# Attention's output normalised ahead of its split, the MLP norm's sum inside the third opening product, and another order of the maxima

## What is computed

```python
def rmsnorm(x, g):
    y = x * lax.rsqrt(jnp.mean(x * x, axis=-1, keepdims=True) + EPS)
    return y * g

def layer_output(x, q_nope, q_pe, pos, ckv_keys, kpe_keys, key_pos, y_lru, p):
    ...
    o = chunk_causal_attention(...)                    # softmax(q k) v, 8 heads of 64
    merged = jnp.concatenate([rmsnorm(o.reshape(B, T, ATTN_W), p["attn_out_g"]),
                              rmsnorm(y_lru, p["lru_out_g"])], axis=-1)
    h = x + merged @ p["w_out"]
    f = jnp.square(jax.nn.relu(rmsnorm(h, p["norm_mlp_g"]) @ p["w_up"])) @ p["w_down"]
    return h + f
```

## Time and profile before

| | us |
|---|---|
| median of 3 runs | 2449.06 (2448.76 to 2449.34) |
| the profiled execution | 2446.93 |
| its span, first to last instruction | 2445.1 |
| PE, DVE, ACT, POOL busy | 2427.2, 1806.5, 1283.4, 537.9 |
| granted TensorE clock, mean | 0.999 of 2.4 GHz |
| attention of the first layer, about | 297 to 457 |
| its Y products | 457 to 501 |
| its output products | 501 to 548 |
| its first MLP products | 548 to 574 |

### The profile page before, as it was taken

The page is one execution under the profiler, slowest core; times in us unless marked ns, Lnnn a source line. Parts: engine busy times, 40 slices in busy tenths (PEclk is TensorE's granted clock), DMA queues, the critical chain, the costliest instruction groups (busy, mean ns, idle before and its releaser), DMA issues. The chain is left out here.

```text
span 2445.1 us, 44182 instructions
## 1 busy us (share of the span) xinstructions
PE 2427.2 (99%) x17358; PEld 2340.8 (96%) x17358; DVE 1806.5 (74%) x2893; ACT 1283.4 (52%) x2306; POOL 537.9 (22%) x513
## 2 busy tenths in 40 slices
PE   9999999999999999999999999999999999999998
PEld 9999977899999999999999999778999999999998
DVE  8677767778776677677686777687787766776676
ACT  5566355655554454455535763557455544554454
POOL 0024155200112211220201142552002112211212
PEclk9999999999999999999999999999999999999999
DMA  4232200453447634664731221005435456546655
GB/s 164 71 115 73 53 11 20 88 154 106 96 86 139 129 84 98 133 120 90 221 100 52 61 73 54 11 20 115 133 109 114 88 115 132 109 87 121 132 104 185
DMA packets 109740, 242.48 MB, mean 99 GB/s; under 512 B 15536, under 2 KB 18960, under 8 KB 109408
## 3 DMA queue, kind: packets, MB, share of 16 engines
q0 software_dynamic: 48512, 102.26, 23.3%
q1 hardware_dynamic: 60880, 137.37, 18.0%
q10 hardware_dynamic: 144, 0.04, 0.0%
HBM read 147.39 MB, written 94.29 MB: 99 GB/s over the span
## 5 line engine op out<-in xcount | busy, mean ns | idle before, releaser
L3270 DVE TENSOR_TENSOR wlo<-raw_all,whi 128x512 fp32r<-128x512 f32 (+1 forms) x420 | 270.6, 653 | 181.1 <-ACT whi L2308 178.6
L2308 ACT ACTIVATE whi<-raw_all 128x512 fp32r<-128x512 f32 (+1 forms) x420 | 248.6, 599 | 278.4 <-DVE raw_all L3403 88.0
L3792 POOL DMA_DIRECT2D x_scratch<-stage x224 | 200.0, 943 | 839.1 <-DVE stage L3413 694.0
L2361 ACT ACTIVATE stage<-ps 128x536 f32<-128x536 f32 (+1 forms) x224 | 135.5, 612 | 148.6 <-PE ps L1590 143.6
L3413 DVE TENSOR_TENSOR stage<-stage,ps 128x536 f32<-128x536 f32 (+1 forms) x168 | 118.9, 708 | 84.8 <-PE ps L1590 84.0
L2873 DVE TENSOR_REDUCE mxp<-ps 128x1 f32<-128x80 f32 (+10 forms) x376 | 137.1, 376 | 51.7 <-PE ps L1304 47.7
L1113 PE MATMUL ps<-xgh,whi 128*128 128x358 f32 (+1 forms) x720 | 157.2, 326 | 0.0
L1113 PE MATMUL ps<-xgl,whi 128*128 128x358 f32 (+1 forms) x720 | 156.6, 325 | 0.0
L1113 PE MATMUL ps<-xgh,wlo 128*128 128x358 f32 (+1 forms) x720 | 156.5, 325 | 0.0
L1738 ACT ACTIVATE whi<-raw_all 128x1024 fp32r<-128x1024 f32 (+3 forms) x64 | 58.1, 908 | 174.5 <-PE ps L1113 158.0
L1113 PEld LDWEIGHTS ps<-xgl,whi 128*128 128x128 f32 x720 | 124.0, 189 | 0.0
(11 more groups left out here) (948 smaller groups left out, 7799.7 us busy)
## 6 DMA issues: line engine op xcount, KB each, us to landing
raw_all<-in_wst SPq DMA_DIRECT2D x237, 256.0 KB, 3.4
raw_all<-in_wst SPq DMA_DIRECT2D x74, 512.0 KB, 3.6
x_scratch<-stage POOLq DMA_DIRECT2D x120, 268.0 KB, 6.1
x_scratch<-stage POOLq DMA_DIRECT2D x120, 264.0 KB, 6.0
xall<-x_scratch SPq DMA_DIRECT2D x32, 537.0 KB, 8.6
x_scratch<-xall POOLq DMA_DIRECT2D x24, 537.0 KB, 3.5
raw_all<-in_wst POOLq DMA_DIRECT2D x30, 256.0 KB, 5.5
xall<-in_xT SPq DMA_DIRECT2D x8, 537.0 KB, 8.4
```

Of the source, the lines that this page charges most:

```text
L2308: nc.scalar.activation(dst, src, ACT.Copy).then_inc(S["u_hi"], 1)
L2361: nc.scalar.activation(quarters(stage_of(L, g, i, n)[:, 0:N2]), src, ACT.Copy, scale=-1.0 if row else 1.0).then_inc(S["x_copy"], 1)
L3270: V.tensor_tensor(dst, src, hi.bitcast(F32), ALU.subtract).then_inc(S["u_lo"], 1)
L3792: pool.dma_start(x_scr[2 * i + row, :, a:b], stage_of(L, g, i, n)[:, 0:b - a], accum_op=ALU.add).then_inc(S[done], 16)
```

## The change

Four things, in both layers.

1. In attention, DVE's copy of bank 1's sums moves from step 12 to step 13, behind `all_parts` and `shift_lo`, and `invert` of heads 2, 4 and 6 from step 10 to step 14. The last reciprocal, after head 7, moves ahead of the first Y weight parts.
2. Attention's output is divided by its root-mean-square before the split: `divide(3)`, the squares and their sum come earlier, PE sums after P7 of pair 2, ACT makes logarithm and root around the copy of P4 of pair 2, DVE multiplies o by the root (`o_normal`, four operations, new), ACT rounds and DVE makes the low parts after that. The output products are then added to x straight from PSUM, one DVE operation each and not two.
3. Some of ACT's PSUM copies in the Y stage stand ahead of weight roundings, others behind.
4. The sum for the MLP norm is made from two fp32r parts (ACT rounds, L2261 of the changed file; DVE makes the rest), after 3 of the 8 tiles of the third opening product.

```diff
+SUM_LAG = [OUT_LAG, OUT_LAG + 1, OUT_LAG]
...
-INVERT_AT = 10
+INVERT_AT = 14
...
 # PE
                     if u in (U_OO, U_OO + 1):
                         w("y_copy", y_copied(u - U_OO + 2, "P4"))
                         w("y_add", y_added(3, "P3"))
-                        w("root", SUM_O)
...
                     if name == "P1":
+                        if p == 3:
+                            w("root", SUM_O)
...
-                        if (p, name) == (NYP - 1, "P7"):
+                        if (p, name) == (2, "P7"):
                             w("sum_lo", SUM_O)
...
                             sum_of_parts(SUM_O, osqt_r, osq_r)
...
-                pe.wait_ge(S["xm_sum"], L * PER["xm_sum"] + 7)
-                sum_of_squares(SUM_MLP, xss)
                 pe.wait_ge(S["u_lo"], L * PER["u_lo"] + 4)
                 pe.wait_ge(S["p_copy"], L * PER["p_copy"] + 2)
-                first_up(2, range(8), True)
+                first_up(2, range(3), False)
+                w("sum_lo", SUM_MLP)
+                sum_of_parts(SUM_MLP, xss_hi, xss_lo)
+                first_up(2, range(3, 8), True)
...
 # ACT, Y stage, from pair 1's P6 on
                 y_copy(1, "P6")
-                o_high(2)
                 y_fill_hi(2, 1)
-                o_square(2)
+                o_square(3)
                 y_fill_hi(2, 2)
                 y_copy(1, "P4")
-                y_fill_hi(2, 3)
+                w("o_sum", 3)
+                nc.scalar.activation(live(osqt_r), live(osq), ACT.Copy).then_inc(S["sum_hi"], 1)
                 y_copy(2, "P1")
-                o_high(3)
+                y_fill_hi(2, 3)
                 y_copy(2, "P5")
                 y_fill_hi(3, 0)
                 y_copy(2, "P6")
-                o_square(3)
                 y_fill_hi(3, 1)
-                y_fill_hi(3, 2)
+                log_sum(SUM_O, rs, ATT)
                 y_copy(2, "P4")
-                y_fill_hi(3, 3)
+                exp_root(SUM_O, rs)
+                y_fill_hi(3, 2)
                 y_copy(3, "P1")
-                w("o_sum", 3)
-                nc.scalar.activation(live(osqt_r), live(osq), ACT.Copy).then_inc(S["sum_hi"], 1)
+                y_fill_hi(3, 3)
+                o_high(0)
+                o_high(1)
                 y_copy(3, "P5")
                 split(B_OO)
                 y_copy(3, "P6")
-                log_rstd(SUM_O, rs, ATT)
+                o_high(2)
+                o_high(3)
                 split(B_OO + 1)
                 y_copy(3, "P4")
...
 # DVE
-                            hb, ib = divmod(h * NP + i - OUT_LAG - BANK_LAST[n_bank], NP)
+                            hb, ib = divmod(h * NP + i - SUM_LAG[n_bank] - BANK_LAST[n_bank], NP)
...
+                def o_normal(j):
+
+                    w("rstd", SUM_O)
+                    w("o_sq", j + 1)
+                    V.tensor_tensor(live(o[j]), live(o[j]), live(rs), ALU.mult).then_inc(S["o_n"], 1)
...
+                divide(3)
                 y_add(1, "P2")
                 y_add(1, "P7")
...
+                o_add(3)
                 y_add(1, "P3")
-                divide(3)
                 y_fill_lo(2, 2)
+                sum_lo(osq_r, osq, osqt_r, SUM_O)
...
                 y_add(2, "P3")
+                o_normal(0)
                 y_fill_lo(3, 2)
+                o_normal(1)
                 y_fill_lo(3, 3)
-                o_low(3)
-                sum_lo(osq_r, osq, osqt_r, SUM_O)
+                o_low(0)
+                o_normal(2)
                 split(B_OO)
+                o_normal(3)
                 y_add(3, "P2")
                 y_add(3, "P7")
+                o_low(1)
                 y_add(3, "P3")
+                o_low(2)
+                o_low(3)
                 split(B_OO + 1)
...
-                    scaled(U_OO + i, osqt, rs, "oo_ev", LIVE)
-                    w("oo_ev", i + 1)
                     w(f"x_in{m}", 32)
-                    V.tensor_tensor(live(x[m]), live(x[m]), live(osqt), ALU.add).then_inc(S["res_add"], 1)
+                    w("mm", U_OO + i + 1)
+                    V.tensor_tensor(chunks(x[m], LIVE), chunks(x[m], LIVE), slot(U_OO + i, LIVE), ALU.add).then_inc(S["res_add"], 1)
```

More of the change, by code:

```diff
@@ L250 @@
 for _c in range(8):
-    READ[U_OO + _c] = ("oo_ev", _c + 1)
+    READ[U_OO + _c] = ("res_add", _c + 1)
 for _c in range(10):
@@ L612, in trunk @@
                 seven[name, kk] = [part[:, h * HALF:(h + 1) * HALF] for part in b_in[m]]
+        xss_lo, xss_hi = place("xss_lo", "G", PIECE * 6, TOK, F32R), place("xss_hi", "G", PIECE * 4, TOK, F32R)
         xss, xsq = place("xss", "G", PIECE * 6, TOK), [place(f"xsq{n}", "G", PIECE * (2 + 2 * n), TOK) for n in range(2)]
@@ L666, in trunk @@
             *((f"x_in{m}", 32) for m in range(8)), ("x_out", 32 * 8), *((f"staged{i}", 0) for i in range(N_STAGE)), ("xg_hi", 8), ("xg_lo", 8), ("sq", 8), ("sq_sum", 7),
-            ("root", 6), ("rstd", 6), ("sum_hi", 5), ("sum_lo", 5),
+            ("root", 6), ("rstd", 6), ("sum_hi", 6), ("sum_lo", 6),
             ("xr_ev", 4), ("xr_raw", 0), ("conv", 4), ("xc_hi", 4), ("xc_lo", 4),
@@ L716, in sum_rest @@
             if n in (SUM_O, SUM_MLP):
-                return ps[:, 1 if n == SUM_O else 5, CH:CH + b - a - SUM_END]
+                return ps[:, 5, CH:CH + b - a - SUM_END]
             return ps[:, 3 * slot_of(sum_at(n, layer)) + 2, CH:CH + b - a - SUM_END]
@@ L1480, in _ @@
                 pe.wait_ge(S["u_lo"], L * PER["u_lo"] + 2)
-                pe.wait_ge(S["oo_ev"], L * PER["oo_ev"] + 7)
+                pe.wait_ge(S["res_add"], L * PER["res_add"] + 7)
                 first_up(0, range(6), False)
-                pe.wait_ge(S["oo_ev"], L * PER["oo_ev"] + 8)
+                pe.wait_ge(S["res_add"], L * PER["res_add"] + 8)
                 first_up(1, range(6), False)
@@ L1809, in log_rstd, with exp_root @@
                     nc.scalar.activation(dst[:, a + SUM_END:b], sum_rest(n, L), ACT.Ln, scale=1.0 / dim, bias=eps[:, 0:1]).then_inc(S["root"], 1)
+                def exp_root(n, dst):
                     w("root", n)
+                    a, b = sum_cols(n, L)
                     nc.scalar.activation(dst[:, a:b], dst[:, a:b], ACT.Exp, scale=-0.5).then_inc(S["rstd"], 1)
+                def log_rstd(n, dst, dim):
+                    log_sum(n, dst, dim)
+                    exp_root(n, dst)
                 w("vec_in", 16)
@@ L2080, in o_high @@
                 def o_high(j):
-                    w("o", j + 1)
+                    w("o_n", j + 1)
                     nc.scalar.activation(live(oh[j]), live(o[j]), ACT.Copy, scale=col(V_AG + j)).then_inc(S["o_hi"], 1)
                 def o_square(j):
+                    w("o", j + 1)
                     if j >= 2:
@@ L2092, in _ @@
                 y_copy(0, "P1")
-                o_high(0)
+                o_square(0)
                 y_copy(0, "P5")
@@ L2096, in _ @@
                 y_copy(0, "P6")
-                o_square(0)
+                o_square(1)
                 y_fill_hi(1, 1)
-                o_high(1)
-                o_square(1)
                 y_copy(0, "P4")
@@ L2104, in _ @@
                 y_fill_hi(1, 3)
+                o_square(2)
                 y_copy(1, "P5")
@@ L2244, in opening @@
                     w("res_add", 8)
+                    w("xm_sum", 7)
+                    nc.scalar.activation(xss_hi[:, A0:TOK], xss[:, A0:TOK], ACT.Copy).then_inc(S["sum_hi"], 1)
                     copy_out(at, 0, True)
@@ L3065, in _ @@
                 y_add(0, "P3")
-                o_low(0)
+                o_add(1)
                 y_fill_lo(1, 2)
                 y_block_sum(2, 0)
-                o_add(1)
                 y_fill_lo(1, 3)
+                o_add(2)
                 y_fill_lo(2, 0)
                 y_block_sum(2, 1)
-                o_low(1)
+                divide(3)
                 y_add(1, "P2")
@@ L3168, in _ @@
                 for i, m in enumerate(OO_ORDER):
-                    if i == 0:
-                        w("rstd", SUM_O)
                     if i == 6:
@@ L3194, in _ @@
                 in_sum(7)
-                for name, kk in F_ORDER[2:]:
+                for name, kk in F_ORDER[2:4]:
+                    seven_sum(name, kk)
+                w("sum_hi", SUM_MLP)
+                lo(xss_lo[:, LIVE[0]:TOK], xss[:, LIVE[0]:TOK], xss_hi[:, LIVE[0]:TOK], "sum_lo")
+                for name, kk in F_ORDER[4:]:
                     seven_sum(name, kk)
```

24 lines of the change are left out of this document (9 added, 15 removed).

## The result

The changed kernel takes 2471.64 us (median, 2470.58 to 2473.03), the kernel before in the same session 2448.76: ratio 1.0095, 95% interval 1.0081 to 1.0109. That is 22.9 us slower. The forecast was slower too, but by 9.2 us (2458.3), and the measured time lies above its range (2451 to 2463) and above every rival, D included.

What follows compares the result with a forecast made beforehand. TensorE, busy 99%, bounds the kernel, so only dropped matmuls or PE waits count. Terms -7.3 -0.4 +8.6 +6.9 +1.1 +0.3 = +9.2 us on the median 2449.06 gave 2458.3, range 2451 to 2463.

Steps and rivals of the forecast that it cites:

- D: few_shifts' tiny transfers queue behind the reciprocal's store and land 0.6 to 1.6 us later: 2462 to 2468 us; chance 0.06.
- Step 1: Attention: the row-sum copy and reciprocal move behind DVE's reduction, so PE's transposes stop waiting; -7.3 us, bounds -5.1 and -7.5.
- Step 2: GpSimd's queue, heads 3, 5, 7: the reciprocal's store delays few_shifts, PE waits 1.43 us each; +8.6 us, bounds 8.0 to 12.2.
- Step 3: Last Y pair: PE waits 1.2 us at P6, 1.8 at P7, 0.4 at output product; +6.9 us, bounds 4 and 8.
- step 4: divide(3) and the squares, moved earlier, delay Y-stage adds that PE waits for; +1.1 us for both layers, bounds 0 and 2.6.
- Step 5: MLP sum: third opening product waits 0.87 us for ACT's copy, two-part sum takes 1.13 against 1.85; +0.3 us.
- the 0.4 us of a late block: Layer 1: weight block B_OO+2, which landed 0.39 us too late, now has 3 us more; -0.4 us.
- A: GpSimd's queue does not bind, so the 8.6 us drop out: 2449.7 us, no change; chance 0.07.
- B: ACT's copies do not stall PE, so the 6.9 us drop out: 2451.4 us, within 0.2%; chance 0.06.
- C: Faster: both queues keep up, and the gains at the transposes, MLP sum and late block stay: 2440.0 us; chance 0.04.

Runs made afterwards that it cites:

- order and few_shifts first: Kernel before with only the maxima's order, and few_shifts issued ahead of store_inverse on GpSimd: 2443.29 us, ratio 0.9982.
- the swap: Changed kernel with few_shifts issued ahead of store_inverse on GpSimd for heads 3, 5 and 7: 2451.58 us, ratio 1.0012.

## Why the prediction was wrong

- **What bounds the kernel, and where PE would wait.** Right. Every new wait of PE over 0.7 us stands at a place that the prediction named.
- **Step 1, the transposes.** Forecast -7.3, measured -4.6 (order and few_shifts first) and -3.9 (the changed kernel with few_shifts first) in attention, outside its bounds. The waits for L2880 all went, but "what is late next no longer stops PE" was wrong: DVE's casts for the next head, which follow its work on the Y operands, were 0.2 us ahead of PE in the kernel before, and PE now arrives earlier. Missed by 3.
- **Step 2, GpSimd's queue.** This is the step that failed. Mechanism and order were right (last issue 3.10 us after the shift, 3.0 forecast), the size was not: +8.6 forecast (bounds to 12.2), +20.5 measured by the swap. Three things make up the difference. The waits of heads 3 and 7 measured 1.54 to 1.85 us idle, 1.7 to 2.0 with the 0.15, and not 1.43; at head 3 the 0.2 KB landed after 1.8 and 1.9 us, inside the row's spread. The wait at head 5 was 3.51 and 4.25, 2.0 us longer in each layer, because DVE's low parts, on which SP's `y_load(2)` waits, were late too: the load fell between the two tiny transfers instead of behind them. Moving it took exactly 2.0 us off both. And the clock: 4 x 1.71 = 6.8 us, which keeping TensorE busy gave back. The sum of idle time (14.6), 0.15 for each of six waits and 6.8 is 22.3; the stretches show 20.5, since the kernel with the swap has 1.3 us more of small waits there (three of them, 0.15 each on top), which the long ones had covered.
- **Where the walk was too short.** Step 2 followed one queue. A move on DVE shifts every queue that waits for DVE, and SP's was one of them, with 512 KB behind it. It treated the landing of 1.6 us as a property of the transfer, though its row held a maximum of 2.2; with the load between them the same transfers took 3.5 to 4.2.
- **Step 3, attention's norm, with step 4.** Right up to the first output product. +6.9 and +1.1 forecast, together 8.0; measured +3.9 and +4.2, 8.1. The last pair of the first layer shows P6 waiting 1.24 us (1.2 forecast) and P7 1.60 (1.8), both at full clock:

```profile
503.00 0.49 PE L1437 MATMUL ps<-yt20h,whi 128*128 128x268 f32 x2 [1.24 <-ACT ystage L2019]
507.84 0.49 PE L1437 MATMUL ps<-yt30h,whi 128*128 128x268 f32 x2 [1.60 <-ACT ystage L2019]
```

  Step 4's share is small and in no list of waits, but the starts show it: counted from the first Y product, P7 of pair 2 starts 0.15 us later than before in the first layer (27.41, 27.26) and 0.43 in the second. That is 0.6 for step 4, 1.1 forecast, and leaves 7.5 for step 3, 0.6 above its value and inside its bounds.
- **Step 5, the MLP's sum, and the 0.4 us of a late block.** The wait was right: the third product waits 0.76 idle and 0.15, 0.91 against 0.87. The sum came out, +0.1 for the rest of the kernel against -0.1 (by the medians some 1.8 less), but partly by luck. "All off the path" was wrong both ways: alone, this part costs 2.3 us and not 0.3, because the low part on DVE delays the activations, and what the norm gives back behind the Y products, some 2.5 us, had no term.
- **The rivals.** A and B are out by the trace. C, faster, would have needed both queues to keep up. D put the late landing down to GpSimd's store; with the store in its place and SP's load moved away the transfers landed after 1.6 and 1.5 us, so it was the load, and D's 2462 to 2468 was still too low, for it had no clock either.
- **The range.** It took only the landing's spread for the bounds of step 2. A wait of PE of 1.4 to 2 us had no cost in it beyond its own length. With the clock behind four of six and the load's 4 us the same walk gives 9.2+6.8+4.0 = +20.0.

## What to carry to other kernels

When an operation is moved on one engine, walk every queue that waits for it, and look for the large transfer that now falls ahead of a small one on which TensorE waits. A wait of TensorE from about 1.8 us on can cost 1.7 us more than its length, in lower clock behind it, so six medium waits are dearer than their sum. And a wait that goes uncovers the next: three times here (the casts, P4, the down products) part or all of a gain turned up again a few products later.

## What the runs showed of the hardware

- A wait of TensorE was followed by half clock, 1.71 us lost, in 0 of 15 cases of 0.54 to 1.6 us, 4 of 9 between 1.76 and 2.25, and 8 of 8 above 3 us. Idle transposes in the wait prevented it.
- A transfer of 0.1 or 0.2 KB issued by GpSimd landed after 1.5 to 1.9 us in most places, and after 3.5 to 4.2 where SP issued 512 KB between the two. What counts is when: with the load issued 1.2 us ahead of them it was 2.2 and 2.8, with 2.5 us ahead 1.6 and 1.7, and with 0.29 us behind them 1.5 and 1.6.
- GpSimd and DVE seem to hold each other up. GpSimd's 800 columns took 3.68 us where 1000 took 2.31 at another head, while DVE's operation on 256 columns took 1.93 us, 0.42 in the changed kernel. By the Trainium skill, SBUF — State Buffer, section "SBUF: two separate sides", the two share a pair of ports that one instruction holds to its end. These rows agree with that in part: at head 4 DVE's multiplication, begun 0.54 us behind the 1000 columns, took 2.89 us, 1.27 elsewhere, but at head 3 DVE's low part, begun 1.33 us behind the 800 columns, took its usual 0.62. No run here tried it apart.
